# A Hyena and mLSTM encoder layer on one core: a ring of three product banks, blocks exchanged and awaited singly, moved loads and first steps, and the spectrum product as one operation

## What is computed

```python
def long_conv(z, ks, d):
    zf = jnp.fft.rfft(z, n=2 * L, axis=1)
    return jnp.fft.irfft(zf * ks[None], n=2 * L, axis=1)[:, :L] + d * z

z = x1.astype(F32) * long_conv(v.astype(F32), kspec[:, 0], bias[0])
return x2.astype(F32) * long_conv(z, kspec[:, 1], bias[1])
...
def encoder_layer(x, ...):
    proj = rmsnorm(x, norm1_g) @ w_in              # then depthwise convolutions of width 3
    y_hy = hyena_mix(x1, x2, hv, kspec, hy_bias)   # two long convolutions, 512 channels
    hm = mlstm_bidir(q, k, v, gates)               # 4 heads x 128, log_sigmoid(gates) inside
    x = x + jnp.concatenate([y_hy, y_ml], axis=-1) @ w_out
    u = dwconv3(rmsnorm(x, norm2_g) @ w_up, ffn_conv_w, ffn_conv_b)
    return x + (jax.nn.silu(gate) * val) @ w_down
```

## Time and profile before

| | |
|---|---|
| median of three runs | 2383.06 us |
| the profiled execution's own time | 2382.36 us |
| its span in the trace | 2380.5 us |
| PE busy | 2253.8 us, 95% |
| DVE busy | 1188.4 us, 50% |
| ACT busy | 785.5 us, 33% |
| mean granted clock of TensorE | 0.983 of full |

### The profile page before, as it was taken

The page is one execution under the profiler, slowest core; times in us unless marked ns, Lnnn a source line. Parts: engine busy times, 40 slices in busy tenths (PEclk is TensorE's granted clock), DMA queues, the critical chain, the costliest instruction groups (busy, mean ns, idle before and its releaser), DMA issues.

```text
span 2380.5 us, 26125 instructions
## 1 busy us (share of the span) xinstructions
PE 2253.8 (95%) x10340; PEld 1862.0 (78%) x10340; DVE 1188.4 (50%) x1655; ACT 785.5 (33%) x1193; POOL 146.4 (6%) x163
## 2 busy tenths in 40 slices
PE   6999999998998979877899999999999999999998
PEld 5788888887886867666788888888888887888886
DVE  6676777645732766657365333343333334324332
ACT  5432333344434434544244212122122123324221
POOL 0221131100111000100000000000000000000000
PEclk8999999999998989999999999999999999999999
DMA  4354544444556566765644111121112112545542
GB/s 143 111 151 131 143 142 129 142 155 159 176 181 205 154 188 180 220 162 159 224 139 169 54 61 51 53 80 62 53 49 69 55 53 102 177 115 171 156 150 85
DMA packets 213588, 307.23 MB, mean 129 GB/s; under 512 B 15480, under 2 KB 143864, under 8 KB 213466
## 3 DMA queue, kind: packets, MB, share of 16 engines
q1 hardware_dynamic: 200858, 256.00, 35.3%
q0 software_dynamic: 11312, 46.14, 5.3%
q10 hardware_dynamic: 1296, 3.41, 0.4%
HBM read 207.38 MB, written 72.16 MB: 117 GB/s over the span
## 4 chain that ended last, share of the span: by engine, by line
PE 51%; DVE 0%; ACT 0%; issue 0%; DVEq 0%; POOL 0%
PE mlp_acc L128 10%; PE mlp_acc L130 10%; PE mlp_acc L129 10%; PE mlp_dacc L128 7%; PE mlp_dacc L130 7%; PE mlp_dacc L129 7%; PE mlp_acc L2596 0%; DVE out_s_lo L2494 0%; DVE up_u L245 0%; ACT up_u L2437 0%; DVE mlp_h_lo L2516 0%; DVE out_w_lo L2489 0%; DVE down_d_lo L2538 0%; ACT out_s_hi L2412 0%; DVE up_u L249 0%
## 5 line engine op out<-in xcount | busy, mean ns | idle before, releaser
L128 PE MATMUL mlp_acc<-mlp_h_hi,up_w_hi 128*128 128x512 f32 x1056 | 411.6, 390 | 0.2 <-DVE mlp_h_lo L2516 0.2
L129 PE MATMUL mlp_acc<-mlp_h_lo,up_w_hi 128*128 128x512 f32 x1056 | 411.4, 390 | 0.0
L130 PE MATMUL mlp_acc<-mlp_h_hi,up_w_lo 128*128 128x512 f32 x1056 | 411.3, 390 | 0.0
L2521 DVE TENSOR_TENSOR up_w_lo<-up_w_raw,up_w_hi 128x1024 fp32r<-128x1024 f32 x44 | 53.8, 1225 | 388.3 <-ACT up_w_hi L2429 388.3
L128 PEld LDWEIGHTS mlp_acc<-mlp_h_hi,up_w_hi 128*128 128x128 f32 x1056 | 198.4, 188 | 41.4 <-DVE mlp_h_lo L2516 0.6
L130 PEld LDWEIGHTS mlp_acc<-mlp_h_hi,up_w_lo 128*128 128x128 f32 x1056 | 198.4, 188 | 41.1
L129 PEld LDWEIGHTS mlp_acc<-mlp_h_lo,up_w_hi 128*128 128x128 f32 x1056 | 198.4, 188 | 40.9
L128 PE MATMUL mlp_dacc<-down_d_hi,down_s_hi 128*128 128x512 f32 x528 | 206.4, 391 | 5.3 <-DVE down_d_lo L2538 5.3
L129 PE MATMUL mlp_dacc<-down_d_lo,down_s_hi 128*128 128x512 f32 x528 | 206.2, 391 | 0.0
L130 PE MATMUL mlp_dacc<-down_d_hi,down_s_lo 128*128 128x512 f32 x528 | 206.2, 390 | 0.0
L2429 ACT ACTIVATE up_w_hi<-up_w_raw 128x1024 fp32r<-128x1024 f32 x44 | 46.6, 1060 | 460.2 <-PE mlp_acc L130 460.2
(11 more groups left out here) (243 smaller groups left out, 3894.1 us busy)
## 6 DMA issues: line engine op xcount, KB each, us to landing
in_w_raw<-arg_w_in_t SPq DMA_DIRECT2D x58, 512.0 KB, 3.7
down_s_raw<-g_scratch SPq DMA_DIRECT2D x48, 512.0 KB, 4.6
up_w_raw<-arg_w_up_t SPq DMA_DIRECT2D x44, 512.0 KB, 3.5
g_scratch<-up_prod POOLq DMA_DIRECT2D x22, 768.0 KB, 3.5
filt_tab<-arg_fwd SPq DMA_DIRECT2D x32, 512.0 KB, 3.8
mix_classes<-mix_split SPq DMA_DIRECT2D x48, 256.0 KB, 8.6
mix_kf<-k_scratch SPq DMA_DIRECT2D x48, 256.0 KB, 2.8
mix_split<-mix_classes SPq DMA_DIRECT2D x48, 256.0 KB, 5.0
```

Source lines behind the costliest of these rows:

```text
L128: pe.matmul(out, w_hi, x_hi, start=first, stop=False)
L129: pe.matmul(out, w_hi, x_lo, start=False, stop=False)
L130: return pe.matmul(out, w_lo, x_hi, start=False, stop=last)
L2521: dve.tensor_tensor(w_lo[i % 2][:, :, :], raw[i % 2][:, :, :], w_hi[i % 2][:, :, :].bitcast(F32), ALU.subtract).then_inc(sem["w_low"], 1)
```

## The change

1. **Three banks.** The bank `gacc` goes, and `vyacc` has three banks, which `split`, `join`, `turn` and now also `inverse` take in turn. A step waits for the release of the use three places back (`vy[-3]`), and `inverse` no longer for the copy of the inverse just before.
2. **Blocks singly.** `to_split` becomes one semaphore per block, and each join waits for its own block. Where all had been implied, waits are added: SP before the first `shuffle_classes` of order 1 of a stream, ACT before the first `copy_turned`.
3. **The first `load` with a `back` in its next eleven steps is moved behind that `back`.**
4. **First steps.** The gap ahead of the pairs shrinks from 6 to 3.2, so that forward steps come earlier among the heads' steps.
5. **Spectrum product.** `kf` holds the spectrum twice, straight and with its two halves of 64 partitions exchanged, by three DMAs (256 KB and twice 128 KB) where there was one. `multiply` is one operation over 128x1024 with `xacc` read twice, instead of one over 128x512 and two over 64x512.
6. **Gates.** `softplus` becomes three planned steps of cost 2.8, and `load_gates` has delay 9.0 in the plan.

```diff
-            return "SP", 1.0, 4.0, [("store", i) for i in gate_tiles] + [("drain_k",)]
+            return "SP", 1.0, 9.0, [("store", i) for i in gate_tiles] + [("drain_k",)]
         if kind == "softplus":
-            return "ACT", 7.5, 0, [("load_gates",)]
+            return "ACT", 2.8, 0, [("softplus", a[0] - 1) if a[0] else ("load_gates",)]
...
-    conv.append(("gap", 6))
+    conv.append(("gap", 3.2))
...
+    for n, step in enumerate(schedule):
+        if step[0] == "load":
+            near = [m for m in range(n, min(n + 12, len(schedule))) if schedule[m][0] == "back"]
+            if near:
+                schedule.insert(near[-1], schedule.pop(n))
+                break
...
-            before["join", args] = vy[-2] if len(vy) >= 2 else None
+            before["join", args] = vy[-3] if len(vy) >= 3 else None
...
+        elif kind == "inverse":
+            before["inverse", args] = vy[-3] if len(vy) >= 3 else None
+            vy.append(("g_copied", args[0] + 1))
...
-    vy_of = {step: n % 2 for n, step in enumerate(x for x in schedule if x[0] in ("split", "join", "turn"))}
+    vy_of = {step: n % 3 for n, step in enumerate(x for x in schedule if x[0] in ("split", "join", "turn", "inverse"))}
...
-                    sp.dma_start(kf[g % ring][:, :, :], k_d[s][o, t, half, :, :, :]).then_inc(k_loaded[g % ring], 16)
+                    sp.dma_start(kf[g % ring][:, 0, :, :], k_d[s][o, t, half, :, :, :]).then_inc(k_loaded[g % ring], 16)
+                    for first in (0, SUB):
+                        sp.dma_start(kf[g % ring][first:first + SUB, 1, :, :], k_d[s][o, t, half, SUB - first:P - first, :, :]).then_inc(k_loaded[g % ring], 16)
...
-                                     ).then_inc(to_split[st], 16)
+                                     ).then_inc(to_split[st][b], 16)
...
-                    if b == 0:
-                        pe.wait_ge(to_split[st], 16 * nts[s] * (o + 1))
+                    pe.wait_ge(to_split[st][b], 16 * (o + 1))
...
-                    x, kk = xacc[g % 2], kf[g % ring]
-                    dve.tensor_tensor(prod[g % 2][:, :, 0, :], x[:, :, :], kk[:, :, :], ALU.mult)
-                    dve.tensor_tensor(prod[g % 2][0:SUB, :, 1, :], x[0:SUB, :, :], kk[SUB:P, :, :], ALU.mult)
-                    dve.tensor_tensor(prod[g % 2][SUB:P, :, 1, :], x[SUB:P, :, :], kk[0:SUB, :, :],
+                    x = xacc[g % 2][:, :, :].rearrange("p u c -> p (u c)").unsqueeze(1).broadcast_to([P, 2, 2 * HC])
+                    dve.tensor_tensor(prod[g % 2][:, :, :, :].rearrange("p i u c -> p i (u c)"), x, kf[g % ring][:, :, :, :].rearrange("p i u c -> p i (u c)"),
                                       ALU.mult).then_inc(sem["multiplied"], 1)
```

More of the change, by code:

```diff
@@ L1532, in long_convolutions_and_heads @@
             v_at[args] = len(v_at)
-            before[args] = vy[-2] if len(vy) >= 2 else None
+            before[args] = vy[-3] if len(vy) >= 3 else None
             vy.append(("v_copied", len(v_at)))
@@ L1540, in long_convolutions_and_heads @@
             t_at[args] = len(t_at)
-            before["turn", args] = vy[-2] if len(vy) >= 2 else None
+            before["turn", args] = vy[-3] if len(vy) >= 3 else None
             vy.append(("copied", len(t_at)))
+        elif kind == "inverse":
+            before["inverse", args] = vy[-3] if len(vy) >= 3 else None
+            vy.append(("g_copied", args[0] + 1))
         elif kind == "keys":
@@ L1567, in long_convolutions_and_heads @@
         split_slot, class_slot = [None, ahead.split1], [None, ahead.classes1]
-        kf = [p.sb(f"kf{b}", [P, 2, HC]) for b in range(ring)]
+        kf = [p.sb(f"kf{b}", [P, 2, 2, HC]) for b in range(ring)]
         og = p.sb("og", [P, T])
@@ L1600, in long_convolutions_and_heads @@
         xacc = [p.ps(f"xacc{b}", [P, 2, HC]) for b in range(2)]
-        gacc = p.ps("gacc", [P, 2, HC])
-        vyacc = [p.ps(f"vyacc{b}", [P, 2, HC]) for b in range(2)]
+        vyacc = [p.ps(f"vyacc{b}", [P, 2, HC]) for b in range(3)]
         bank = {x: p.ps(f"bank_{x}", [P, CH]) for x in "abc"}
@@ L1609, in long_convolutions_and_heads @@
         z_loaded, y_stored, tab_loaded, head_stored = ahead.z_loaded, ahead.y_stored, ahead.tab_loaded, ahead.head_stored
-        to_classes, to_split = ([p.sem(f"{x}{st}") for st in range(len(streams))] for x in ("to_classes", "to_split"))
+        to_classes = [p.sem(f"to_classes{st}") for st in range(len(streams))]
+        to_split = [[p.sem(f"to_split{st}_{b}") for b in blocks(st)] for st in range(len(streams))]
         k_loaded = [p.sem(f"k_loaded{b}") for b in range(ring)]
@@ L1652, in shuffle_classes @@
                     sp.wait_ge(sem["v_copied"], v_at[o, st, b] + 1)
+                    if (o, b) == (1, 0):
+                        for back in to_split[st]:
+                            sp.wait_ge(back, 16)
                     if (o, st, b) == (0, 1, 0):
@@ L1816, in inverse @@
                     pe.wait_ge(sem["multiplied"], g + 1)
-                    if g:
-                        pe.wait_ge(sem["g_copied"], g)
+                    free(before["inverse", (g,)])
+                    out = vyacc[vy_of["inverse", g]]
                     for u in range(2):
                         for i in range(2):
-                            last = pe.matmul(gacc[:, u, :], tab[s][:, t, u, 1 + i, :], prod[g % 2][:, u, i, :],
+                            last = pe.matmul(out[:, u, :], tab[s][:, t, u, 1 + i, :], prod[g % 2][:, i, u, :],
                                              start=i == 0, stop=i == 1)
@@ L1913, in copy_turned @@
                     act.wait_ge(sem["transposed"], t_at[st, b] + 1)
+                    if b == 0:
+                        for back in to_split[st]:
+                            act.wait_ge(back, 16 * ORDER)
                     for x in range(HC // P):
@@ L1976, in multiply @@
                 def multiply(g):
[L1977 removed]
+                    dve.wait_ge(k_loaded[g % ring], 48 * (g // ring + 1))
                     dve.wait_ge(sem["x_ready"], g + 1)
```

23 lines of the change are left out of this document (13 added, 10 removed).

## The result

The changed kernel takes 2365.27 us (median of six runs, 2363.53 to 2374.35) against 2386.18 for the kernel before on the same chips. The ratio is 0.9919, with a 95% interval of 0.9898 to 0.9939: 19 us faster (15 to 24), where 37 were forecast. The profiled execution took 2363.53 us, its span is 2361.7.

What follows compares the result with a forecast made beforehand. Stage 2 was taken as bound by latencies around an in-order PE. Terms of -9, -22, -9, -4, +2 and +2 made -40; 3 given back left -37 from 2382.4, so 2345 us, range 2322 to 2368.

Steps and rivals of the forecast that it cites:

- gates: Softplus in stage 1: three steps close PE's 7.88 us hole, -9 us, bounds 0 and -10.
- blocks singly, load moved: Stage 2 joins: three exchange waits of 17.6 us go, with lower clock behind them, -22 us, bounds -12 and -24.
- three banks: Stage 2 joins and splits: most of 12.2 us of waits on banks go, -9 us, bounds 0 and -12.
- start (gap): First forward, moved ahead of the links, waits about 10 us for the first exchange: +2 us, bounds -3 and +6.
- product: DVE's spectrum product in one operation shortens PE's waits for the last product: -4 us, bounds 0 and -5.6.
- more transfers: 96 more spectrum DMAs, 12.6 MB, in stage 2, mostly hidden: +2 us, bounds 0 and +12.
- gave back 3 us: PE arrives early at waits once hidden, above all the heads' chains and the load of z: 3 us returned.
- Rival 2: Stage 2 spectra come too late, so every pair waits and the kernel is slower: 2398 us, chance 0.06.
- what is late next: Stream 2 exchange: the head's data and the spectrum loads behind it come later, with some 14 us before their use.
- Rival 1: Most gain is given back to the heads' chains and crowded transfers: -15 us, 2367 us, chance 0.18.

Runs made afterwards that it cites:

- e9: The kernel before with only the gates' part (softplus in three planned steps, delay 9.0): 2374.89 us, ratio 0.9952.
- e10: The kernel before with only the semaphores by block, their waits, and a head's load moved behind the exchange back: 2386.01 us, ratio 1.0001.
- e1: The changed kernel with the old spectrum product: one 256 KB load per spectrum and three DVE operations: 2354.64 us, ratio 0.9863.
- e15: e1 without the block semaphores and without the loop that moves the load: 2355.10 us, ratio 0.9869.
- e13: e10 with the head's load put two forward steps further on: 2375.47 us, ratio 0.9959.
- e11: The kernel before with only the ring of three banks taken in turn by split, join, turn and inverse: 2373.55 us, ratio 0.9947.
- e16: The kernel before with only the gap ahead of the pairs at 3.2: 2381.12 us, ratio 0.9981.
- e7: The changed kernel with rows 0 to 63 of each spectrum stored once more, both copies loaded as 256 KB over 128 partitions: 2351.03 us, ratio 0.9857.
- e12: e7 with the gap ahead of the pairs back at 6: 2360.27 us, ratio 0.9888.
- e3: The changed kernel with the three loads kept and awaited, but the three old product operations on the straight copy alone: 2379.16 us, ratio 0.9965.
- e6: As e3, everything loaded, but DVE's product waits for the straight copy alone: 2371.76 us, ratio 0.9933.
- e5: As e3, but the two extra loads bring only 16 elements of each row: 2359.47 us, ratio 0.9890.
- e8: As e7, but both copies fetched by one 512 KB load: 2353.74 us, ratio 0.9862.

## Why the prediction was wrong in size

The direction was right, and the waits that were to go went; the sum of -37 became -19. Term by term, predicted and measured:

| term | predicted | measured | from |
|---|---|---|---|
| gates | -9 | -11 | e9 |
| blocks singly, load moved | -22 | 0 alone, -1 in the whole, -10 alone with the load further on | e10, e1 and e15, e13 |
| three banks | -9 | -13 | e11 |
| start (gap) | +2 | -5 alone, -7 on e7 (with the loop's move) | e16, e7 and e12 |
| product | -4 | -11 | e3 and the change |
| more transfers | +2 | +24 | e1 and e3 |

The prediction gave back 3 us besides. With -1 and -5 the measured terms add to -17; the whole is -19.

**Two steps failed, by 22 and 21 us: "More transfers", +2 for a measured +24, and "Blocks awaited singly, and a load moved", -22 for a measured -1.** That the whole missed by 18 us only is because the start, the product and the banks came out better. On the transfers I wrote that with three DMAs "I expect 4 us, hidden". The landing was 5 to 5.7 us of each, and not hidden: the 8.1 us that the ring gives were taken from the last product to its use in a steady stretch, while the loads are issued by SP in order, behind exchanges and heads. The upper bound of +12 was too low as well, since it left out what the bytes do to other transfers (e6). What would have shown it was named: "I am wrong if DVE waits for spectra in many pairs". Rival 2 had the kind of mechanism, spectra that come too late, but in every pair and in step at a landing of 12 us, and asked for 0.9 us a pair; they were late in ten of 48 pairs, and the loads took 24 / 48 = 0.5. The rule that I weighed against the row, of the Trainium skill ("DMA: Bandwidth & Descriptors", Rules for kernel authors), that transfers over disjoint partition halves serialize and one over 128 partitions is to be used, pointed the right way. By that rule the trace agrees that halves are no gain, and goes further: they took 57 us of the engines' time where full width took 30, and e7 is 15 us faster. The landing that I took from it, near three in a row (8.4 to 9.3 us), did not come: it was 5.7.

**Blocks singly** failed as a price for removed waits. The trace did what I said, the three waits went. But I counted them as path. The 5.8 us of stream 1, order 0, were slack of a round of two exchanges, 40 us long with or without them, and with the 2.6 of order 1 taking them away is worth nothing that can be told (1 us, e15 against e1). The 9.2 us of stream 2 went by the gap, not by the edit to which I gave them. The sentence on what is late next, spectra "behind it" with "some 14 us" in hand, was false: the trace of the kernel before had DVE waiting 8.10 us for such a spectrum at that place, a row that the sum left out, and in e10 it is PE's 10.85 us. Rival 1 had this mechanism, with the term at -12, never at nothing; that its sum of 2367 us is close to the 2365 is chance, since the loss sits in the transfers.

**The start** had the sign wrong. The wait there was as forecast (9.9 us, the first forward at 755.48, which is 763 less the 7.7 us of stage 1), but the same number decides where a later load falls.

**The gates and the banks** were 2 and 4 us better than forecast, no more than their errors. **The product** took 1.22 us as estimated from the earlier trace rows, and was worth 11 us and not 4. I take it that a shorter product also pulls in all that waits behind it on DVE, above all after a late spectrum; no run shows that apart. With transfers at full width, new product and loads together are even with the old ones (e7 against e1, 0.9857 and 0.9863).

The fastest version is e7, 2351 us, 15 us under the changed kernel; e1 is as fast within the errors with 12.6 MB fewer to move.

Open stays through which transfers the 10 us of e6 over e5 act, beyond the later landing of the straight copy, and why the product with its loads costs 13 us in the whole change and nothing alone.

## What to carry to other kernels

Before counting a removed wait as gain, look whether another engine waits at the same time for something later in the same queue, and follow the round to the next point that the same transfers release: if the distance there is set by two exchanges, the wait only changes its place. In an in-order DMA queue the price of a moved or added load is what stands behind it, and here an operand that a third engine awaits in order was what came late. Where a schedule is merged by a credit, print where the large loads fall after each edit; a number at its start may do what a rule written for it no longer does.

## What the hardware showed that I had not expected

- The same bytes as two DMAs over 64 partitions took twice the time of the DMA engines that they took over 128: 57 us against 28 to 30, for 12.6 MB more, as 96 halves or at full width (e7, e8).
- Two DMAs of 4 KB beside each spectrum cost 6 us over 48 pairs (just clear of the errors), with 2.7 us to landing, hardly less than a full one's 2.9 in the same kernel.
- A DVE operation of 128x1024 that reads one PSUM bank twice took 1.22 us, no more than the same size on SBUF.
